# A hybrid encoder layer with 32 experts: the last expert's second layer by column halves instead of row halves

## What is computed

```python
h   = layer_norm(alpha * x + mix, ln1_w, ln1_b)
# each token: the 4 best of 32 experts, softmax weights over those 4
glu, lin = split(h_e @ w1[e] + b1[e])                 # w1: 1024 x 2048 for each expert
a   = min(glu, 7) * sigmoid(1.702 * min(glu, 7)) * (clip(lin, -7, 7) + 1)
y_e = a @ w2[e] + b2[e]                               # w2: 1024 x 1024 for each expert
ffn = sum over the token's experts of weight * y_e
out = layer_norm(alpha * h + ffn, ln2_w, ln2_b)
```

## Time and profile before

| what | value |
|---|---|
| time of 3 runs | median 1294.64 us (1293.88 to 1295.3) |
| the profiled execution | 1294.97 us, of which the span is 1293.2 us |
| granted TensorE clock over the span | 0.996 |
| busy: PE / PEld / DVE / ACT / POOL | 1247.0 (96%) / 635.1 (49%) / 453.4 (35%) / 218.8 (17%) / 3.5 us |
| HBM read | 457.53 MB, mean 355 GB/s over the span, 425 to 437 GB/s in most slices of the expert stage |
| chain that ended last | PE 67%, DMA 23%, DVE 7%, ACT 1%, issue 1% |

### The profile page before, as it was taken

One profiled execution on the slowest core, in us unless ns is written; L12 is line 12 of the kernel. 1 busy time (PEld: TensorE's weight loads), 2 busy tenths in 40 slices (PEclk: granted clock), 3 DMA queues, 4 the chain that ended last, 5 costly groups with the idle time before them and its releaser, 6 DMA issues.

```text
span 1293.2 us, 14907 instructions
## 1 busy us (share of the span) xinstructions
PE 1247.0 (96%) x6082; PEld 635.1 (49%) x6082; DVE 453.4 (35%) x910; ACT 218.8 (17%) x428; POOL 3.5 (0%) x17
## 2 busy tenths in 40 slices
PE   9999999999999999999999899999998999999996
PEld 8888888998753333333333233333323333333331
DVE  5999924456353412121221212122121312222123
ACT  1722124131040110101101010110101010110102
POOL 0000000000000000000000000000000000000000
PEclk9999999999999999999999999999999999999999
DMA  9533334326889999999999999999999999999995
GB/s 378 201 131 135 125 138 164 122 106 238 344 323 402 427 431 434 426 435 429 429 432 430 430 430 431 430 434 426 433 433 425 437 427 431 435 426 428 427 425 222
DMA packets 30286, 459.52 MB, mean 355 GB/s; under 512 B 4592, under 2 KB 4976, under 8 KB 9360
## 3 DMA queue, kind: packets, MB, share of 16 engines
q1 hardware_dynamic: 26656, 453.00, 83.5%
q10 hardware_dynamic: 3568, 5.59, 1.2%
HBM read 457.53 MB, written 1.05 MB: 355 GB/s over the span
## 4 chain that ended last, share of the span: by engine, by line
PE 67%; DMA 23%; DVE 7%; ACT 1%; issue 1%; SPq 0%; DVEq 0%; POOL 0%; POOLq 0%
DMA store<-in_moe_w 23%; PE banks L1222 16%; PE banks L822 15%; PE banks L1256 12%; PE banks L836 4%; PE banks L1228 3%; PE banks L1099 2%; DVE store L1908 2%; PE banks L1315 2%; PE banks L1156 1%; DVE store L1905 1%; DVE store L1902 1%; DVE store L1907 1%; PE banks L1238 1%; ACT store L714 1%
## 5 line engine op out<-in xcount | busy, mean ns | idle before, releaser
L1222 PE MATMUL banks<-store 128*64 128x512 f32 x1536 | 344.6, 597 | 19.5 <-DMA store<-in_moe_w 14.1
L1222 PEld LDWEIGHTS banks<-store 128*64 128x64 f32 x1536 | 109.8, 137 | 237.5 <-issue 215.4
L1256 PE MATMUL banks<-store 128*64 128x512 f32 x952 | 210.9, 595 | 0.0
L822 PE MATMUL banks<-store 128*128 128x256 f32 x896 | 196.7, 380 | 0.0
L822 PEld LDWEIGHTS banks<-store 128*128 128x128 f32 x896 | 169.4, 190 | 26.0 <-issue 3.5
L1902 DVE TENSOR_SCALAR store<-banks 128x512 f32<-128x512 f32 x32 | 22.1, 691 | 431.7 <-PE banks L1228 431.7
L1256 PEld LDWEIGHTS banks<-store 128*64 128x64 f32 x952 | 65.7, 137 | 143.1 <-issue 118.7
L1228 PE MATMUL banks<-store 128*64 128x512 f32 x512 | 116.8, 598 | 1.4 <-DMA store<-in_moe_w 1.4
L1916 DVE COPY store<-banks 64x512 f32<-64x512 f32 x30 | 20.8, 694 | 213.6 <-PE banks L1256 213.6
L714 ACT ACTIVATE store<-store 128x512 f32<-128x512 f32 x29 | 18.3, 630 | 449.2 <-DVE store L1902 449.2
L1228 PEld LDWEIGHTS banks<-store 128*64 128x64 f32 x512 | 34.2, 136 | 71.3 <-issue 68.6
(11 more groups left out here) (378 smaller groups left out, 835.0 us busy)
## 6 DMA issues: line engine op xcount, KB each, us to landing
store<-in_moe_w SPq DMA_DIRECT2D x72, 4096.0 KB, 34.9
store<-in_moe_w SPq DMA_DIRECT2D x43, 2048.0 KB, 15.0
store<-in_w_in SPq DMA_DIRECT2D x30, 1024.0 KB, 4.9
store<-in_moe_w SPq DMA_DIRECT2D x9, 1024.0 KB, 38.9
store<-in_w_branch SPq DMA_DIRECT2D x8, 1024.0 KB, 4.8
store<-in_w_out SPq DMA_DIRECT2D x4, 1024.0 KB, 6.1
store<-in_w_first SPq DMA_DIRECT2D x2, 512.0 KB, 5.8
store<-in_xT ACTq DMA_DIRECT2D x2, 512.0 KB, 6.3
```

The lines of the kernel that those rows point to most:

```text
L822: last = mm(b[:, j * SEQ:(j + 1) * SEQ], w[:, k, j * P:j * P + P], xT[:, k, :], start=k == 0, stop=k == KD - 1)
L1222: last = mm(bank[i][64 * ct:64 * ct + 64, :], xg[:, 2 * c + kk, col:col + CAP], w[:, kk, i * FF + ct * 512:i * FF + ct * 512 + 512], start ...
L1256: last = mm(bank[4][64 * dh:64 * dh + 64, :], actT[:, j, 64 * fh:64 * fh + 64], w[j][:, 512 * dh:512 * dh + 512], start=(fh, j) == (0, 0), ...
```

## The change

Only the second layer of expert 31 and what follows it are touched.

- **SP.** The four pieces of expert 31 are cut by columns: piece (c4, d0) is rows 0 to 3 of unit 4, columns 0 to 511, as [128 x 4 x 512], so a partition's share is four runs of 2 KB. Order: (c4, d0), (c5, d0), (c4, d1), (c5, d1). They still have 1 MB each. The waits for the ring's places that stood between them now stand before the first.
- **PE.** `last_columns(c, dh)` takes one piece: four products, all in the column half `dh`; `dh` = 0 goes to bank 0, partitions 0 to 63, and `dh` = 1 to bank 1, partitions 64 to 127. `last_combine(i, dh)` issues the two products of one column half after that half's copy alone. The first combination (expert 30) stands after one piece instead of two.
- **ACT and DVE.** Both copies of expert 31's result are ACT's now; the left one is asked for when both pieces d0 are done. Expert 30's copies stay divided. The semaphores `ypair_act`, `ypair_vec` become `ypair_lo`, `ypair_hi`.
- **DVE at the end.** The addition goes in four pieces of 512 columns, columns 0 to 511 of both token halves first, each with its own row sum; the small scaling adds two sums.

```diff
@@ sync
-                else:
+                elif e == NE - 2:
                     for j in range(2):
                         part = slice(SLOT * j, SLOT * j + SLOT)
                         sp.dma_start(tail_at(e, c)[:, part], unit_source(e, c)[:, part]).then_inc(late_landed[late(e, c, j)], 16)
+            for dh in range(2):
+                for c in range(NW1, NU):
+                    sp.dma_start(columns(tail_at(NE - 1, c), dh), columns(unit_source(NE - 1, c), dh)).then_inc(late_landed[late(NE - 1, c, dh)], 16)
@@ scalar
-            second_out(0, bank[4])
-            second_out(1, bank[0])
+            last_out(0, 0, bank[4], LAST + 4)
+            last_out(1, 0, bank[0], LAST + 5)
+            last_out(1, 1, bank[1], LAST + 6)
@@ tensor
+            def last_columns(c, dh):
+
+                pe.wait_ge(late_landed[late(NE - 1, c, dh)], 16)
+                w = columns(tail_at(NE - 1, c), dh)
+                fh = c - NW1
+                for k in range(4):
+                    last = mm(bank[dh][64 * dh:64 * dh + 64, :], actT_last[:, k, 64 * fh:64 * fh + 64], w[:, k, :],
+                              start=(fh, k) == (0, 0), stop=(fh, k) == (1, 3))
+                if fh:
+                    last.then_inc(S["expert_chunk_used"], 1)
...
+            def last_combine(i, dh):
+
+                pe.wait_ge(S["ypair_lo"] if dh == 0 else S["ypair_hi"], NE - 1 + i)
+                r = 64 * dh
                 for half in range(2):
...
+                    last = mm(bank[COMB_BANK[2 * half + dh]][:, :], wselT_last[i][r:r + 64, half, :], y_last[i][r:r + 64, :],
+                              start=i == 0, stop=i == 1, tile_position=(r, 0))
+                    if i == 1:
+                        last.then_inc(S["comb_psum"], 1)
...
-            second_half_unit(1, NW1, 0, actT_last, bank[0])
-            second_half_unit(1, NW1, 1, actT_last, bank[0])
-            last_combine(0)
-            second_half_unit(1, NW1 + 1, 0, actT_last, bank[0])
-            second_half_unit(1, NW1 + 1, 1, actT_last, bank[0])
-            last_combine(1)
+            last_columns(NW1, 0)
+            pe.wait_ge(S["wselT_ready"], NPAIR)
+            last_combine(0, 0)
+            last_combine(0, 1)
+            last_columns(NW1 + 1, 0)
+            last_columns(NW1, 1)
+            last_columns(NW1 + 1, 1)
+            last_combine(1, 0)
+            last_combine(1, 1)
@@ vector
-            for half in range(2):
-                total = banks[:, COMB_BANK[2 * half]:COMB_BANK[2 * half] + 2, :]
-                dve.wait_ge(S["comb_psum"], NPAIR * 4 + 2 * half + 2)
-                link(V.scalar_tensor_tensor(rows(half), total, 1.0, rows(half), ALU.mult, ALU.add, accum_out=small[:, 300 + half:301 + half]))
-                V.tensor_scalar(small[:, 302 + half:303 + half], small[:, 300 + half:301 + half], -1.0 / D, None, ALU.mult).then_inc(S["sum_ready"], 1)
+            for dh in range(2):
+                for half in range(2):
+                    piece = y_acc[:, half, 512 * dh:512 * dh + 512]
+                    dve.wait_ge(S["comb_psum"], NPAIR * 4 + 2 * dh + half + 1)
+                    link(V.scalar_tensor_tensor(piece, bank[COMB_BANK[2 * half + dh]], 1.0, piece, ALU.mult, ALU.add,
+                                                accum_out=small[:, 316 + 2 * half + dh:317 + 2 * half + dh]))
+                    if dh == 1:
+                        V.tensor_scalar(small[:, 302 + half:303 + half], small[:, 317 + 2 * half:318 + 2 * half], small[:, 316 + 2 * half:317 + 2 * half],
+                                        -1.0 / D, ALU.add, ALU.mult).then_inc(S["sum_ready"], 1)
```

More of the change, by code:

```diff
@@ L360, in late, with columns @@
             return 4 * (e - NE + 2) + 2 * (c - NW1) + j
+        def columns(v, dh):
+            return v.rearrange("p (k n) -> p k n", k=4)[:, :, 512 * dh:512 * dh + 512]
         ln2_w, ln2_b = unit_at(LAST - 4)[:, 0:D], unit_at(LAST - 4)[:, D:2 * D]
@@ L721, in expert @@
                 act.wait_ge(S["expert_chunk_used"], n * NU + NU)
-                nc.scalar.activation(y_pair[64 * u:64 * u + 64, 0:512], bank[4][0:64, :], ACT.Copy).then_inc(S["ypair_act"], 1)
+                nc.scalar.activation(y_pair[64 * u:64 * u + 64, 0:512], bank[4][0:64, :], ACT.Copy).then_inc(S["ypair_lo"], 1)
             def sigmoid(n):
@@ L745, in _ @@
             act.wait_ge(S["expert_chunk_used"], NU)
-            nc.scalar.activation(y_pair[0:64, 0:512], bank[4][0:64, :], ACT.Copy).then_inc(S["ypair_act"], 1)
+            nc.scalar.activation(y_pair[0:64, 0:512], bank[4][0:64, :], ACT.Copy).then_inc(S["ypair_lo"], 1)
             with act.Fori(0, NPAIR - 2) as p:
@@ L750, in _, with last_out @@
             expert(NE - 3, 1, NPAIR - 2, NPAIR - 1)
-            def second_out(i, src):
-                act.wait_ge(S["expert_chunk_used"], LAST + 4 + 2 * i)
-                nc.scalar.activation(y_last[i][0:64, :], src[0:64, :], ACT.Copy).then_inc(S["ypair_act"], 1)
+            def last_out(i, dh, src, used):
+                act.wait_ge(S["expert_chunk_used"], used)
+                nc.scalar.activation(y_last[i][64 * dh:64 * dh + 64, :], src[64 * dh:64 * dh + 64, :], ACT.Copy)\
+                    .then_inc(S["ypair_hi"] if dh else S["ypair_lo"], 1)
             sigmoid(NE - 2)
@@ L1268, in weights, with second_half_unit @@
                 last.then_inc(S["wselT_psum"], 1)
-            def second_half_unit(i, c, j, turned, b):
-                pe.wait_ge(late_landed[late(NE - 2 + i, c, j)], 16)
-                w = tail_at(NE - 2 + i, c).rearrange("p (k n) -> p k n", k=4)
+            def second_half_unit(c, j):
+                pe.wait_ge(late_landed[late(NE - 2, c, j)], 16)
+                w = tail_at(NE - 2, c).rearrange("p (k n) -> p k n", k=4)
                 fh = c - NW1
@@ L1276, in second_half_unit @@
                     for dh in range(2):
-                        last = mm(b[64 * dh:64 * dh + 64, :], turned[:, k, 64 * fh:64 * fh + 64], w[:, k, 512 * dh:512 * dh + 512],
+                        last = mm(bank[4][64 * dh:64 * dh + 64, :], actT[:, k, 64 * fh:64 * fh + 64], w[:, k, 512 * dh:512 * dh + 512],
                                   start=(fh, k) == (0, 0), stop=(fh, k) == (1, 3))
                 if j:
+                    last.then_inc(S["expert_chunk_used"], 1)
[7 more added lines that the diff above has]
+                if fh:
                     last.then_inc(S["expert_chunk_used"], 1)
@@ L1308, in combine @@
                     pe.wait_ge(S["wselT_ready"], m_ + 1)
-                    pe.wait_ge(S["ypair_act"], n)
-                    pe.wait_ge(S["ypair_vec"], n)
+                    pe.wait_ge(S["ypair_lo"], n)
+                    pe.wait_ge(S["ypair_hi"], n)
                     if combined is not None:
@@ L2005, in _ @@
             swiglu(NE - 1, 1, last_expert=True)
-            for i in range(2):
-                dve.wait_ge(S["expert_chunk_used"], LAST + 4 + 2 * i)
-                V.tensor_copy(y_last[i][64:128, :], bank[4 * (1 - i)][64:128, :]).then_inc(S["ypair_vec"], 1)
+            dve.wait_ge(S["expert_chunk_used"], LAST + 4)
+            V.tensor_copy(y_last[0][64:128, :], bank[4][64:128, :]).then_inc(S["ypair_hi"], 1)
             dve.wait_ge(S["comb_used"], NPAIR * 4)
```

12 lines of the change are left out of this document (5 added, 7 removed).

## The result

| | before | after |
|---|---|---|
| median of the runs taken side by side (6 each), us | 1294.26 | 1299.2 |
| lowest to highest, us | 1293.8 to 1295.3 | 1298.33 to 1299.39 |
| ratio, 95% interval | | 1.0033 (1.0023 to 1.0043) |
| profiled execution, us | 1294.97 | 1299.13 |
| its span, us | 1293.2 | 1297.4 |

The changed kernel is slower by 0.33% (the two medians alone lie 4.94 us apart, 0.38%); on the median of 1294.64 that the forecast started from, 0.33% gives 1298.9. The forecast said slower by 2.57 us (1297.2). The direction is right, the size is not: the span grew by 4.2 us, and 1.6 us of that are in no term of the sum. 1298.9 lies just beyond the range, which ended at 1298.8; the interval of the ratio, 1297.6 to 1300.2 on the same median, has that edge inside it.

The account below looks back on a forecast made before the run. PE was taken to bound the last 8 us: it ends 3.01 us later, 0.44 is gained from there to L2051, sum +2.57 us, so 1297.2 against a median of 1294.64. Range 1296.2 to 1298.8.

Parts of the forecast that it names:

- 1284.3: Sign in the changed kernel's profile: the prediction is wrong if PE ends its pieces before 1282.5 or after 1284.3.
- (c4, d0) usable: Landing of expert 31's first column piece: 1270.49 plus 0.25 us for 2 KB runs, so 1270.74.
- Rival 2: Weight stream: 2 KB runs cost up to 0.5 us a piece, PE ends at 1284.04, +3.3, 1297.9; chance 0.12.
- The rule that the prediction set beside this term: Piece transfers: 512 B suffices for line rate, so 2 KB runs cost nothing and the sum would be 0.25 us less.
- Eight steps alone: PE on the first column piece, one half alone: eight steps, 3.65 us, of which the next shape saves 0.07.
- Rival 3: PE: a column half alone runs at twice the pace, first piece 1.94 us; +0.1, 1294.7; chance 0.06.
- First combination: Expert 30's combination on PE: 1.92 us, to 1276.24; order 0, 0, 1, 1 costs nothing if PE looks past.
- (c5, d0) abreast with (c4, d1): PE's second and third pieces overlap on different halves; with the last piece 7.09 us, to 1283.33.
- Rival 1: PE: no overlap of halves across pieces, eight steps or 3.44 us more; +6.0, 1300.6; chance 0.08.
- From PE's end to the norm: Copy, combination, additions and scalings behind PE's last piece, up to L2051: 4.36 us against 4.80, a gain of 0.44.
- SP's queue: SP's moved waits cost nothing; the norm's weights land at 1281.3, three microseconds before DVE needs them (1282.3 at 0.5 us each).

## Why the prediction was right and wrong

PE ended its pieces at 1284.79 (1275.94 + 8.85), past the 1284.3 that the prediction named as a sign of being wrong. In the order of its path:

- *(c4, d0) usable.* Forecast 1270.74, measured 1270.47. The price of 2 KB runs was set at 0.25 us a piece from two lone transfers; in the stream it is 0.16, and here the stream stood 0.18 earlier besides. Rival 2 needed 0.27 and is out. The rule that the prediction set beside this term, from the Trainium skill, "DMA: Bandwidth & Descriptors", Specifications (line rate from 512 B on, so no cost), is not what the runs show either: 5.22 us for two pieces, not 4.90.
- *Eight steps alone.* Forecast 3.58 to the combination, measured 3.55 (1270.47 to 1274.02). Rival 3, a lone half at twice the pace, is out.
- *First combination.* Forecast 1.92, measured 1.92. All eight matmuls overlap in the order 0, 0, 1, 1 too: four in a row for each half of the rows, just what a part holds.
- *(c5, d0) abreast with (c4, d1).* **This step failed.** The prediction took from L936 that "PE looks past matmuls that stand in front for another part of the array". It does so only as long as each part has room for four. L936 has four in a row for a quarter, the combination four for a half; (c5, d0) has eight. The stretch was set at 7.09 us and took 8.85: 1.76 us too little here, and the other terms together were 0.18 too much. Rival 1, with eight steps late and 1300.6, was wrong as well: the truth lay halfway, at four steps. The direction held because another step was right: a half alone takes a full step for each matmul. That 1298.9 lies only 0.1 beyond the range is luck: the range's upper part stood there for rival 2, dearer transfers, which did not come.
- *From PE's end to the norm.* Forecast 4.36, measured 4.48 (the stretch's end, 1284.79, to 1289.27). The small scaling has two operations now, reads a second value for each partition, and takes 0.21 instead of 0.15; what follows it starts 0.13 behind its start where the sum had 0.07, and that twice is the 0.12.
- *SP's queue.* Forecast no cost, and none shows: DVE has the norm's weights at 1280.69, long before its first addition at 1285.95.

Together: -0.27 - 0.03 + 1.76 + 0.12 = 1.58, which is 4.15 less the 2.57 of the sum. Nothing else is open at this size.

The whole difference of 4.17 us can be split by the rows as well. PE's steps from F to the end of the pieces went from 16 to 28 (8 alone, 4 alone, 16 of the right half): 12 x 0.43 = 5.16. From F to the pieces' end it is 14.32 (1270.47 to 1284.79) where it was 9.83 (1270.49 to 1280.32), 4.49 more, so 0.67 came back: before, PE waited 0.45 for the second piece's landing, and the first piece had a tail of 0.22 of its own (1.94 for four steps of 0.43) that the longer row of work now hides. Behind the pieces 4.80 became 4.48, 0.32 less: the additions by columns cost 0.64, and the left half, which was copied long before, gives 0.96 back by covering the right half's copy. 5.16 - 0.67 - 0.32 = 4.17.

The Trainium skill says in "TensorE: Matmul & The Clock Gate", Part 3, that matmuls stay in program order, start and end. For the hand-out, every order tried here fits that. For the starts the runs show otherwise: at 1277.71 the right half's first matmul starts together with the fifth of the left, ahead of three that stand before it in the program. In the kernel after, PE at that moment, with the left half's fourth still running:

```profile
1277.28 1.08 PE L1297 MATMUL banks<-store 128*64 128x512 f32 x3
```

## What to carry to other kernels

When matmuls use only a part of the array, let neighbours in the program go to different parts, and don't put more than four (counted as the trace records them; a float32 product is two) for one part in a row: in these runs each one more cost a full step on the part that waited behind it. This is shown for float32 matmuls of 512 columns on the two column halves, each with its own weight load; rows of four also overlapped on quarters (L936) and on row halves (the combination), and longer rows were not tried there. If a transfer is cut so that its piece feeds one part alone, this order is lost, and a piece that stands alone takes almost twice as long (3.62 us, before 1.94). Where a trace shows that matmuls overlap, count how many stood in a row there before the rule is taken over to a longer row.

## What the runs showed of the hardware that was not expected

- Four matmuls in a row for a half cost nothing (3.67 us for a unit against 3.65), six cost two steps (8.00 against 7.09), eight four (8.85 and 8.86 against 7.09; 6.30 against 4.54).
- A wait between two pieces that had landed cost nothing that can be seen: 8.85 us with it, 8.86 without.
- The two halves' matmuls start out of program order: the right half's first together with the left half's fifth, when eight of the left stand ahead of it (1277.71).
- 1 MB in runs of 2 KB takes 0.16 us longer in the stream than in runs of 8 KB (5.22 against 4.90 for two).
- The same small DVE operation on one value a partition takes 0.21 us with two operations and a second value read, and 0.15 with one operation; which of the two differences costs the 0.06 was not tried.
